# Memory attention of prompt tiles 2 to 7 moved into the programs of the expert stage, with streamed weights, a gather ring of 11 slots and sets of 2 rows

## The reference, cut to what matters

```python
x  = x + merged @ w_out                               # merged: 2048 columns, w_out 2048 x 1024
q  = (rmsnorm(x) @ w_mq) in 4 heads x 256             # read of a memory of 256 rows
x  = x + (softmax(q mk^T / 16) mv) @ w_mo
xn = rmsnorm(x)                                       # gain norm_ffn_w
# PEER experts: 8 heads; per head two lists of 128 key scores, the 16 best of each list,
# the 16 best of their 256 sums -> 16 expert numbers and a softmax over them: 128 experts per token
act = gelu(sum_d peer_u[idx] * xn)                    # per token and expert
x  = x + sum_e gate_e * act_e * peer_v[idx_e]
y  = rmsnorm(x)                                       # gain final_norm_w
```

## Time and profile before

| what | value |
|---|---|
| median of 3 runs | 4848.45 us (4846.26 to 4853.11) |
| the profiled execution: its own time, span | 4845.6 us, 4843.8 us |
| `memory_read` from first load to last store | 1273.7 to 1883.5 us |
| `memory_read_sample` | 1887.3 to 2026.3 us |
| `expert_mix`, first load; first and last gather of the prompt | 2029.2; 2066.2 and 4769.6 us |
| busy over the span | PE 83%, DVE 52%, POOL 30%, ACT 24% |

### The profile page before, as it was taken

How to read it: one execution, slowest core, us unless ns; L and a number is a source line. 1 busy time by engine, 2 the same in 40 slices (tenths; PEclk the granted TensorE clock), 3 DMA queues, 4 the chain that set the end, 5 groups by cost and what they waited for, 6 DMA issues and landing times.

```text
span 4843.8 us, 41636 instructions
## 1 busy us (share of the span) xinstructions
PE 4020.5 (83%) x12109; PEld 2088.0 (43%) x12109; DVE 2506.8 (52%) x5490; ACT 1165.2 (24%) x3569; POOL 1437.6 (30%) x1297
## 2 busy tenths in 40 slices
PE   8998688887799997778888787888778888778877
PEld 4565344443366563344444333444334443334432
DVE  2332454553411111377887654787555787545665
ACT  2332122222011110123333222233222323222322
POOL 0000132330000000044444444444444434444442
PEclk9887799888899999789999899999899999999998
DMA  4001000003601102399999999999999999999997
GB/s 181 18 17 50 15 9 17 17 4 116 249 22 43 43 13 87 129 388 419 415 419 419 420 422 421 413 413 413 417 421 415 408 415 413 421 421 416 417 412 296
DMA packets 210786, 1267.56 MB, mean 262 GB/s; under 512 B 23353, under 2 KB 39774, under 8 KB 76161
## 3 DMA queue, kind: packets, MB, share of 16 engines
q0 software_dynamic: 148608, 1082.20, 54.0%
q1 hardware_dynamic: 62008, 183.44, 10.1%
HBM read 1236.00 MB, written 31.63 MB: 262 GB/s over the span
## 4 chain that ended last, share of the span: by engine, by line
DMA 30%; PE 8%; DVE 7%; issue 5%; POOL 3%; ACT 2%; DVEq 2%; ACTq 0%; POOLq 0%
DMA ex_ring<-in_expert_uv,ex_idx 29%; PE psum L2612 7%; POOL ex_ring L2548 3%; DVE ex_ring L2846 3%; ACT ex_diag L2701 1%; DVEq L2848 1%; PE psum L2591 1%; ACT ex_weight L2696 1%; DVE ex_match L2811 0%; DVE ex_match L2807 0%; DVE ex_joined L2814 0%; DVE ex_best_at L2788 0%; DVE ex_top_at L2772 0%; DVE ex_match L2790 0%; DVE ex_top_at L2764 0%
## 5 line engine op out<-in xcount | busy, mean ns | idle before, releaser
L2612 PE MATMUL psum<-ex_ring,ex_diag 128*128 128x512 f32 x4096 | 1995.2, 644 | 475.5 <-ACT ex_diag L2701 475.3
L2846 DVE CUSTOM_DVE_ANT_0 ex_ring<-ex_ring,ex_x_rows 128x1024 f32<-128x1024 f32 x1024 | 1236.3, 1225 | 840.0 <-DMA ex_ring<-in_expert_uv,ex_idx 809.3
L2548 POOL DMA_INDIRECT ex_ring<-in_expert_uv,ex_idx x1024 | 1207.5, 1179 | 1529.2 <-PE psum L2612 1148.1
L2612 PEld LDWEIGHTS psum<-ex_ring,ex_diag 128*128 128x128 f32 x4096 | 826.1, 207 | 1551.2 <-issue 971.7
L2692 ACT ACTIVATE ex_dots<-ex_dots 128x4 f32<-128x4 f32 x256 | 52.6, 205 | 1649.6 <-DVEq L2848 1649.4
L2701 ACT ACTIVATE ex_diag<-ident,ex_weight 128x128 f32<-128x128 f32 x1024 | 327.2, 390 | 17.9 <-PE psum L2612 0.3
L1023 PE MATMUL psum<-w_zx,ssd_hT 128*128 128x512 f32 (+1 forms) x768 | 297.1, 542 | 3.4 <-issue 1.8
L2591 PE MATMUL psum<-ex_xT,ex_w_q 128*128 128x256 f32 (+1 forms) x1280 | 267.5, 363 | 6.3 <-ACT ex_xT L2664 6.3
L2591 PEld LDWEIGHTS psum<-ex_xT,ex_w_q 128*128 128x128 f32 x1280 | 228.3, 193 | 65.9 <-issue 41.5
L1910 PE MATMUL psum<-w_out,read_mT 128*128 128x512 f32 x512 | 233.4, 606 | 1.7 <-DVEq L2071 0.9
L2696 ACT ACTIVATE ex_weight<-ex_gates,ex_dots 128x1 f32<-128x1 f32 x1024 | 217.7, 283 | 18.5 <-issue 1.1
(11 more groups left out here) (427 smaller groups left out, 3740.6 us busy)
## 6 DMA issues: line engine op xcount, KB each, us to landing
ex_w_q<-in_route_wq SPq DMA_DIRECT2D x80, 512.0 KB
ex_ring<-in_expert_uv,ex_idx POOLq DMA_INDIRECT x1024, 28.5
w_zx<-in_w_in SPq DMA_DIRECT2D x1, 10304.0 KB, 29.5
ex_x_rows<-scratch_xn SPq DMA_DIRECT2D x17, 512.0 KB, 8.8
w_out<-in_w_out SPq DMA_DIRECT2D x2, 4096.0 KB
read_mixed<-scratch_mixed SPq DMA_DIRECT2D x8, 1024.0 KB, 4.7
w_out<-in_cache_mem_k SPq DMA_DIRECT2D x8, 1024.0 KB, 12.1
w_qkv<-in_w_in SPq DMA_DIRECT2D x3, 2048.0 KB, 15.8
```

Of the source, the lines that this page charges most:

```text
L2548: nc.gpsimd.indirect_dma_start(out=ring[:, n % RING, :], out_offset=None, in_=io["expert_uv"], in_offset=bass.IndirectOffsetOnAxis(ap=idx[ ...
L2612: ins = nc.tensor.matmul(psum[2 * (tile % 2) + c][:], diag[:, q % 2, s, :], ring[:, n % RING, D + c * BANK:D + (c + 1) * BANK], start=(n % ...
L2846: nc.vector.tensor_tensor_reduce(ring[:, n % RING, 0:D], ring[:, n % RING, 0:D], x_rows[:, tile % (2 * GT), :], 1.0, 0.0, ALU.mult, ALU.ad ...
```

## The change

`memory_read` keeps tiles 0 and 1 (`READ = 2`). For tiles 2 to 7 the same work is written into `expert_mix`, two tiles at a time (g = 1, 2, 3), in about 112 pieces each. The unit of all programs in `expert_mix` is now a turn of two slots (`SET = 2`, 512 turns, 64 per tile); a few turns with negative numbers route the first heads. Group g's pieces run from turn 0, 120 and 248 (`READ_AT`), the routing of group g from turn -17, 111, 231, 359 and 424 (`ROUTE_AT`, the last is the samples'). With r the turn within a group: r 0 to 7 transposes of the mixed rows, r 9 to 40 the `w_out` products (two program matmuls of 128x512 per turn), r 44 and 45 transposes, r 48 to 63 queries (four of 128x256 per turn), r 64 to 79 scores, softmax and values, r 82 to 97 the `w_mo` products, r 99 to 106 sums and norm. DVE writes the normed rows straight into `x_rows`.

The weights no longer lie in SBUF: SP streams rows of `w_out`, of a re-laid `w_mq` (`read_wq`) and of `w_mo` in chunks of 512 KB, 32 per group, through four buffers that the routing's query weights share (176 chunks in all: 80 looks and 96 of the reads). A chunk is loaded two turns after the use of the one four before it, once PE has counted that use. `mkT` and `mv` now live until the end. To make room, the ring has 11 slots, `x_rows` three tiles rather than four, the result rows one tile rather than two, and the mix one pair of PSUM banks rather than two: PE's first mix of a tile waits until DVE has added the tile before (`total`, in the new tile's second turn). `memory_read_sample` streams its values through five places. The samples' rows and expert numbers are prepared 12 to 16 turns before the end, and the eight rows for their products are loaded into eight places at once.

```diff
-def memory_read_sample(nc, io, psum, shared, w_out, w_mq, w_mo, mkT, mv, x1):
+            for t in range(READ):
+                turn(t, t + 1 if t + 1 < READ else None, first=(t == 0))
+            ffn_rows(READ - 1)
+
...
         loaded, turned, mT_ready, summed, x1_ready = (sem("rs_" + n) for n in ("loaded", "turned", "mT_ready", "summed", "x1_ready"))
         x1_turned, hT_ready, ms_ready, rstd_ready, projected, q_ready = (
             sem("rs_" + n) for n in ("x1_turned", "hT_ready", "ms_ready", "rstd_ready", "projected", "q_ready"))
         spread, q_wide_ready, reduced = sem("rs_spread"), sem("rs_q_wide_ready"), sem("rs_reduced")
         k_in = [sem(f"rs_k_in{b}") for b in range(DEC)]
-        v_in = [sem(f"rs_v_in{i}") for i in range(6)]
...
-    SET = 4
-    SETS = TOPK // SET
+    RING = 11
+    SET = 2
+    CHUNKS = 4
+    HEAD_TURNS = TOPK // SET
+    TILE_TURNS = SLOTS // SET
+    TURNS = TILES * TILE_TURNS
     LOOKS = 2 * PEER_HEADS
-    AHEAD = 2
     OWN = DEC // 2
+    READ_AT = {1: 0, 2: 120, 3: 248}
+    ROUTE_AT = {0: -17, 1: 111, 2: 231, 3: 359, 4: 424}
+    FIRST = ROUTE_AT[0] - 4
+    OUT_AT, ASK_AT, BACK_AT = 9, 48, 82
+    READ_CHUNKS = 4 * DB
+
+    def first_use():
+
+        uses = [(ROUTE_AT[g] + 8 * h + 2 * i, 0, ("look", g * LOOKS + 2 * h + i))
+                for g in ROUTE_AT for h in range(PEER_HEADS) for i in range(2)]
+        for g, at in READ_AT.items():
+            uses += [(at + OUT_AT + 2 * b, 1, ("read", (g - 1) * READ_CHUNKS + b)) for b in range(2 * DB)]
+            uses += [(at + ASK_AT + 2 * d, 1, ("read", (g - 1) * READ_CHUNKS + 2 * DB + d)) for d in range(DB)]
+            uses += [(at + BACK_AT + 2 * b, 1, ("read", (g - 1) * READ_CHUNKS + 3 * DB + b)) for b in range(DB)]
+        return sorted(uses)
...
+    def loads_at(turn):
+
+        return [n for n in range(CHUNKS, len(uses)) if uses[n - CHUNKS][0] + 2 == turn]
...
         ring = sb("ex_ring", [P, RING, 2 * D])
+        chunk = sb("ex_chunk", [P, CHUNKS, D])
         idx, gates = sb("ex_idx", [P, 2, GT, SLOTS], U32), sb("ex_gates", [P, 2, GT, SLOTS])
-        x_rows = sb("ex_x_rows", [P, 2 * GT, D])
+        x_rows = sb("ex_x_rows", [P, 3, D])
...
+            def load_chunk(n):
+
+                if n >= CHUNKS:
+                    kind, i = uses[n - CHUNKS][2]
+                    if kind == "look":
+                        sp.wait_ge(q_full, i + 1)
+                    else:
+                        sp.wait_ge(read_chunks, i + 1)
+                kind, i = uses[n][2]
+                if kind == "look":
+                    i = i % LOOKS
+                    src = io["route_wq"][i * P:(i + 1) * P, :]
+                else:
+                    i = i % READ_CHUNKS
+                    if i < 2 * DB:
+                        src = io["w_out"][i * P:(i + 1) * P, :]
+                    elif i < 3 * DB:
+                        i -= 2 * DB
+                        src = io["read_wq"][i * P:(i + 1) * P, :]
+                    else:
+                        i -= 3 * DB
+                        src = io["w_mo"][i * P:(i + 1) * P, :]
...
+            for turn in range(FIRST, TURNS):
+                for n in loads_at(turn):
+                    load_chunk(n)
+                for back, i in ((5, 2), (7, 3)):
+                    head = head_at(turn, back)
+                    if head is not None and 2 * head + i < (GROUPS + 1) * LOOKS:
+                        load_keys(2 * head + i)
+                g, r = read_at(turn)
+                if r == -6:
+                    load_mixed(g, 0)
+                    load_mixed(g, 1)
+                if r in (3, 4):
+                    load_mixed(g, r - 1)
+                if r == 10:
+                    load_x1(g)
+                if r in (101, 102):
+                    store_x2(g, r - 101)
...
+            for turn in range(TURNS):
+                head, i = turn // HEAD_TURNS, turn % HEAD_TURNS
+                tile, h = head // PEER_HEADS, head % PEER_HEADS
                 g, a = tile // GT, tile % GT
+                if i == 0:
+                    pool.wait_ge(idx_ready, g * PEER_HEADS + h + 1)
+                    pool.sem_inc(gathers, 1)
+                for s in range(SET):
+                    n = turn * SET + s
                     if n >= RING:
                         pool.wait_ge(mixed, n - RING + 1)
...
+                group, r = read_at(turn)
+                if r == 54:
+                    read_root(group, mean1, rstd1, mean1_ready, rstd1_ready)
+                if r == 108:
+                    read_root(group, mean2, rstd2, mean2_ready, rstd2_ready)
...
-                tile = q * SET // SLOTS
+                tile = q // TILE_TURNS
                 pe.wait_ge(diag_ready, q + 1)
-                if q * SET % SLOTS == 0 and tile >= 2:
-                    pe.wait_ge(summed, tile - 1)
+                if q % TILE_TURNS == 0 and tile:
+                    pe.wait_ge(summed, tile)
                 for s in range(SET):
...
                     for c in range(2):
-                        ins = nc.tensor.matmul(psum[2 * (tile % 2) + c][:], diag[:, q % 2, s, :], ring[:, n % RING, D + c * BANK:D + (c + 1) * BANK],
+                        ins = nc.tensor.matmul(psum[c][:], diag[:, q % 3, s, :], ring[:, n % RING, D + c * BANK:D + (c + 1) * BANK],
                                                start=(n % SLOTS == 0), stop=(n % SLOTS == SLOTS - 1), skip_group_check=True)
                     ins.then_inc(mixed, 1)
...
+                if OUT_AT <= r < OUT_AT + 4 * DB:
+                    b, a = (r - OUT_AT) // 2, (r - OUT_AT) % 2
+                    w = chunk[:, chunk_of["read", m * READ_CHUNKS + b] % CHUNKS, :]
+                    if a == 0:
+                        chunk_ready("read", m * READ_CHUNKS + b)
+                    if b == 0:
...
+                    for c in range(2):
+                        ins = nc.tensor.matmul(psum[2 + 2 * a + c][:], mT[:, b, a * P:(a + 1) * P], w[:, c * BANK:(c + 1) * BANK],
+                                               start=(b == 0), stop=(b == 2 * DB - 1), skip_group_check=True)
+                    if a:
+                        ins.then_inc(read_chunks, 1)
...
+                if ASK_AT <= r < ASK_AT + 2 * DB:
+                    d, half = (r - ASK_AT) // 2, (r - ASK_AT) % 2
+                    w = chunk[:, chunk_of["read", m * READ_CHUNKS + 2 * DB + d] % CHUNKS, :].rearrange("p (b n) -> p b n", b=DB)
+                    if half == 0:
+                        chunk_ready("read", m * READ_CHUNKS + 2 * DB + d)
...
+                    for b in range(4 * half, 4 * half + 4):
+                        ins = nc.tensor.matmul(psum[2 + d % 4][:, 0:N], w[:, b, :], hT[:, b, :],
+                                               start=(b == 0), stop=(b == DB - 1), skip_group_check=True)
+                    if half:
+                        ins.then_inc(read_chunks, 1)
...
+            for turn in range(FIRST, TURNS):
+                if turn >= 0:
+                    mix(turn)
+                if turned_at(turn, 0) is not None:
+                    turn_rows(turned_at(turn, 0))
+                for back in range(4):
+                    head = head_at(turn, back)
                     if head is not None:
-                        if i % 2 == 0:
+                        ask(2 * head + back // 2, back % 2)
+                for i in range(2):
+                    head = head_at(turn, 4 + 2 * i)
+                    if head is not None:
+                        score(2 * head + i)
+                g, r = read_at(turn)
+                if g is not None:
...
+                if 67 <= r < 71:
+                    i = r - 67
+                    n, a = i // 2, i % 2
+                    act.wait_ge(peak_ready, 4 * m + i + 1)
...
+                        nc.scalar.activation(p[:, a, h, :], psum[2 + i][:, e * N_MEM:(e + 1) * N_MEM], ACT.Exp,
+                                             bias=peak[:, a, h:h + 1], scale=scale[:, a:a + 1], accum_out=total_p[:, a, h:h + 1])
...
+            def product(n):
+
...
+                if s == 0 and q >= 8:
+                    dve.wait_ge(diag_ready, q - 7)
+                dve.wait_ge(row_in[n % RING], 16 * (n // RING + 1))
+                nc.vector.tensor_tensor_reduce(ring[:, n % RING, 0:D], ring[:, n % RING, 0:D], x_rows[:, tile % 3, :], 1.0, 0.0,
+                                               ALU.mult, ALU.add, dots[:, q % 8, s:s + 1])
+                if s == SET - 1:
+                    dve.drain()
+                    dve.sem_inc(dotted, 1)
...
+                if r in (42, 43):
+                    a = r - 42
+                    dve.wait_ge(read_chunks, m * READ_CHUNKS + 2 * DB)
...
+                        nc.vector.tensor_tensor(x1[:, a, cols], psum[2 + 2 * a + c][:], x1[:, a, cols], ALU.add)
+                    dve.drain()
+                    dve.sem_inc(x1_ready, 1)
...
+            for turn in range(FIRST, TURNS):
+                if turn >= 0:
```

(74 more changed lines are left out.)

665 lines of the change are left out of this document (410 added, 255 removed).

## The result

The changed kernel takes 4556.4 us (median of 4 runs, 4553.0 to 4559.6); the kernel before took 4849.4 beside it (4846.3 to 4853.1). The ratio is 0.9395, 95% interval 0.9379 to 0.9412. Predicted were 4588 us and a range of 4540 to 4715. The profiled execution's own time is 4555.4 us, its span 4553.6; against before's 4845.6 and 4843.8 that is 290.2 us less.

A forecast was written before the change was run, and what follows sets the result against it. Two bounds in sequence: PE in `memory_read`, then the DMA engines in `expert_mix`. 4845.6 - 440.0 removed + 160 DMA + 25 PE - 6 at the end = 4584.6, with the median's offset 4588 us; range 4540 to 4715.

The forecast's parts named there:

- first rival: PE never ends last in `expert_mix`, reading disappears under DMA, SP's bytes go at full rate: 4546 us; chance 0.14.
- likeliest case: The forecast itself, chance 0.55, spanning 4565 to 4625 us with DMA 144 to 175 and PE 0 to 50.
- Removed, -440.0: In `memory_read`, six of seven turns with a front stage go, 73.3 us each, 440.0 us.
- Added on DMA, +160: In `expert_mix`, 60.3 MB more on the DMA engines cost 160 us, taken between 144 and 175.
- my bounds of 345 and 418: GB/s for the added bytes in `expert_mix`: 418 of a full stretch gives 144 us, 345 for SP's bytes gives 175.
- My sign against the byte term: The byte term is wrong if reading turns move under 405 GB/s at a full DMA share.
- Added on PE, +25: In `expert_mix`, 10 us waiting for tile sums, two times 3.2 us at half clock, 8 us in softmax turns.
- The softmax turns, to which I gave 8 us: ACT table loads put 12 turns of the reading about 0.7 us each beyond DMA's pace, 8 us.
- By itself this costs nothing: In reading-and-routing turns PE ends last by 0.16 us, 5 us in 32 turns; the ring lets PE catch up.
- second rival: PE ends last in all reading turns, at clock 0.91: 155 us in place of 25, 4718 us; chance 0.22.
- third rival: Ring too short: a gather's 24.9 us landing is its own transfer time, not queueing; 4900 us, slower; chance 0.05.
- The end, -6: At the samples' products, loading the rows ahead brings the last product's start from 24.2 us towards 17.4: -6 us.

## Why the prediction was right

The time lies in the range, and the two main terms hold: what was removed, and bytes as the price of what was added. It is 32 us below the forecast, and the first rival's 4546 came nearer. The band given for the likeliest case, 4565 to 4625, misses it too; by that band's own terms (DMA 144, PE 0) it begins at 4546.

- **Removed, -440.0.** The first gather is 440.8 us earlier after the 3.4 that belong to earlier stages. The turn without a front took 1436.80 - 1383.21 = 53.6 us (forecast 53.4). From the samples' first load to the first load of `expert_mix` it is 143.4 us instead of 142.0, so five places cost at most 1.4 us.
- **Added on DMA, +160.** The gathers took 163.6 us longer, 154.8 counted to the last product. The packet records have 1188.3 MB between the first and the last gather instead of 1125.6. The 62.7 MB more are 150.6 us at before's mean rate of 416.4 GB/s; the rest is a mean rate of 414.5. All of it put on the 60.3 MB, they went at 369 to 390 GB/s, between my bounds of 345 and 418. That 160 is so near is partly luck, since it was only the middle of the two. The Trainium skill, "HBM Reference", Specifications (TRN2), says that a core streaming alone reaches about 425 GB/s, bounded by its 16 DMA engines. The 418 to 422 of the full stretches agree. My sign against the byte term, under 405 GB/s in reading turns at a full DMA share, seems met by the 402 and 398 of two spells. But these contain the dips, and without the dips they are 414 and 412.
- **Added on PE, +25.** This is the term that was mis-sized: neither run that lightened PE gave anything back, so the parts of it that they test are 0. Its mechanisms were there (waits of 7.48 and 7.24 us at turns 128 and 256, a first mix of 5.57 us instead of 3.60 behind the former). But the DMA engines kept work through the waits, which the prediction had charged in full. The softmax turns, to which I gave 8 us, take 5.13 us, less than any other kind with reading pieces. The query and `w_mo` pieces were not lightened by themselves.
- **How near PE stood.** I had 6.2 us for PE and 6.04 for DMA in turns with reading and routing; they are 6.125 and about 6.14. "By itself this costs nothing" held. The second rival (4718 us) needed PE at clock 0.91; it was 0.97 to 1.00 in these spells, and only the kernel with doubled `w_out` work came near its time (4690). The first rival had PE right, and lost 10 us because it took the bytes at the full rate.
- **Ring.** The third rival fell with the landing of 10.6 us at 8 slots. Held time is 14.2 us against 13.7 in the prediction. That 11 slots cost nothing was tested in the old order alone, where they cost 6.4 us.
- **The end, -6.** The last sample product began 4529.04 - 4511.66 = 17.4 us after the first, as worked out, and the last store came 5.7 us earlier behind the last prompt product. The end as a whole is only 0.8 us shorter, for the 4.9 us behind that store. The 9.6 us from the last gather on contain 8.8 that come from fewer gathers in flight.
- PE waited for no chunk. What I had not listed are its waits for mixed rows, 11.8 us in six.

The errors add up: -0.8 and -3.4 at the front, -30.2 in the stage to the last product (154.8 against 185), +5.2 behind it are -29.2; the profiled execution was predicted at 4584.6 and took 4555.4.

## What to carry to other kernels

Where a stage is bound by transfers and the one ahead of it by matmuls, laying one beside the other costs little more than the added bytes at the stage's own rate (150.6 of 163.6 us here), as long as PE's time per turn does not pass DMA's. Here the two were level, and one more pair of matmuls in 96 turns cost 134 us. A dip in the mean DMA share is not yet lost time: take the pause away and look at the whole. A ring's slots times the pace must exceed what a slot is held plus an unqueued landing by a good margin: with sets of four, 8 x 2.64 = 21.1 us against 14.2 + 6.0 = 20.2 lost 449 us, and 11 x 2.64 = 29.0 lost 6.4.

## What the runs showed of the hardware

The mean rate of the DMA engines falls to 25 GB/s, a sixteenth, when the gathers end: for 10 us in the changed kernel and for 11 us in the kernel before, at 4781 to 4792 us (4765 to 4805 us in 40 slices):

```profile
DMA  9999999999999982000000000008599999999999
GB/s 418 418 442 434 401 401 459 426 418 401 410 442 434 401 344 123 33 25 25 25 33 25 25 25 33 25 25 131 188 410 418 369 385 352 418 410 410 410 434 459
```

One engine is that far behind the others after a long stream of gathers. The DMA share runs ahead of the rate below saturation: in the kernel before with 8 slots it was 0.90 while only 358 GB/s were moved (2700 to 3100 us), in the changed kernel with doubled PE work 0.92 at 353.
